# Three expert groups ranked by load and packed into 32-row lanes: sixteen expert blocks become thirteen in a decoder trunk on one Trainium2 core

## The chip, the core and the metric

The kernel runs on one core of one Trainium2 chip. The metric is device time in microseconds (us), the median of the runs shown. The engines are named as in the profile: PE is TensorE's matmul side, PEld its weight load, DVE is VectorE, ACT is ScalarE, POOL is GpSimd, SP is SyncE, whose queue issues most of the DMAs.

## What is computed

One decoder layer for 512 prompt tokens and 64 sample tokens, 576 in all, with D = 1024: a combined projection, windowed attention beside RWKV-7 time mixing, an output projection with LayerNorm, and a routed mixture of 16 experts. The change touches only the last part:

```
probs = softmax(x @ w_router);  sel = probs + router_bias        # 16 experts, 4 groups of 4
best  = the group whose two best sel have the greatest sum
idx   = the two best experts inside that group                    # 2 rows of work per token
h     = silu(x @ w_gate[e]) * (x @ w_up[e])                       # 1024 -> 512, f32
out   = sum over the two experts of weight * (h @ w_down[e])      # 512 -> 1024, f32
x     = LayerNorm(ALPHA * x + out)
```

Worked out with the reference on its own inputs, the rows that the router gives to each expert are, by group and from the most to the least loaded: 105, 91, 71, 61; then 92, 80, 73, 39; then 86, 71, 58, 53; then 91, 75, 56, 50.

## The kernel before

Up to about 530 us the projection, attention, RWKV and output projection run; then the router picks experts, and 16 expert blocks follow, one for each expert, each with room for CAP = 128 rows. Every engine runs a program of its own, ordered by semaphores.

The routing. DVE makes one-hot masks M1 and M2 of the first and second choice and hands their sum to PE ("chosen" 1). PE counts by matmul how many earlier tokens chose the same expert (L1086 and L1088). DVE turns each count into a row number (L1931 to L1935: for each choice a multiply, a reduce and a comparison with 128 row numbers, which gives a one-hot OH). PE multiplies OH by the token numbers TI (L1096, 20 matmuls), so that each slot of each expert's block learns its token, and DVE casts that to integers (L1939, "slots" 1). POOL then gathers the rows of one block at a time from HBM (L520, 0.5 MB each).

The expert blocks on PE. `gate_up(e)` (L1120) runs 8 matmuls with the gate weights and 8 with the up weights, each of 128 rows by 512 columns in f32, for which the trace shows two instructions each. `turn_xg(e+1)` (L1108) transposes the next block's rows, `down(e-1)` (L1139) multiplies the block before by its down weights, and `turn_h(e)` (L1128) transposes the hidden rows. The order in the loop is gate_up(e), turn_xg(e+1), down(e-1), turn_h(e). ACT and DVE copy and multiply what lies between, and ACT stores a block's 128 result rows to HBM (L1472).

The weights. Each expert has three matrices of 2 MB. WG, WU and WD have two buffers each, expert e uses buffer e % 2. SP issues the loads in one order written in the program (`load_expert`, L439): gate(e), up(e), down(e), gate(e+1) and so on. The loads of experts 0 and 1 are issued before the routing. Each later one first waits until the buffer's last reader is done:

```
            def load_expert(e, s, ahead=True):
...
                for nm, W, src in (("gate", WG, i_["w_gate"]), ("up", WU, i_["w_up"]), ("down", WD, i_["w_down"])):
                    if ahead:
                        sp.wait_ge(sem(nm + "_ps"), e - 1)
                    w = src[0, bass.ds(e, 1)] if ahead else src[0, e:e + 1]
```

The wait for e - 1 is over once blocks 0 to e - 2 have used that matrix. Since down(e-2) runs after gate_up(e-1), down(e), gate(e+1) and up(e+1) go out together. They have most of a block of PE's time before they are read.

After the last block POOL gathers each token's two result rows (L560), DVE combines and normalises, and SP stores the output. If an expert has more rows than its place, all engines run a loop of OVER further blocks behind a flag; with the loads above no expert has.

Of the kernel before, what the change touches and what calls it, by code (L numbers as in the profile page):

```python
# [15 lines left out]
P = 128  # L16
D = 1024
# [14 lines left out]
OVER = 2 * NT // (CAP + 1)  # L32
BLOCKS = E + OVER
# [15 lines left out]
def constant_table():  # L49
# [35 lines left out]
    t_["rank"] = np.tile(np.arange(float(P)), (P, 1))  # L85

    tok = np.arange(5)[None, :] * P + i[:, None]
    t_["tok_high"] = (tok // 32 * 32).astype(float)
    t_["tok_low"] = (tok % 32).astype(float)
    t_["iota4"] = np.tile(np.arange(4.0), (P, 1))  # L90
    t_["slot0"] = np.tile(np.arange(E) * float(CAP), (P, 1))
# [24 lines left out]
def hymba_step(nc, i_, o_):  # L116

    with ExitStack() as ctx:
# [114 lines left out]
        PR, SEL, CN, O1, O2, EQ, M1, M2, PO = (small(5, E) for _ in range(9))  # L233
# [7 lines left out]
        OH = [small(5 * P // 2).bitcast(BF16).rearrange("p (i c) -> p i c", i=5) for _ in range(2)]  # L241
        TI = [small(5 * E).bitcast(BF16).rearrange("p (i h e) -> p i h e", i=5, h=2) for _ in range(2)]
        CH = small(3 * E).bitcast(BF16).rearrange("p (i e) -> p i e", e=E)
        BEF, ONE = (small(P // 2).bitcast(BF16) for _ in range(2))
        smalli = ctx.enter_context(nc.sbuf_tensor("smalli", [P, 10 + BLOCKS + 1 + OVER], I32))
# [3 lines left out]
        eid_i = smalli[:, 11 + BLOCKS:11 + BLOCKS + OVER]  # L249
        x1d = nc.dram_tensor("x1_rows", [NT, D], F32).ap()  # L250
# [114 lines left out]
        def _(sp):  # L365
# [67 lines left out]
            def load_expert(e, s, ahead=True):  # L433

                for nm, W, src in (("gate", WG, i_["w_gate"]), ("up", WU, i_["w_up"]), ("down", WD, i_["w_down"])):
                    if ahead:
                        sp.wait_ge(sem(nm + "_ps"), e - 1)
                    w = src[0, bass.ds(e, 1)] if ahead else src[0, e:e + 1]
                    sp.dma_start(W[s], w.rearrange("a (k p) n -> p (a k) n", p=P)).then_inc(sem(f"w{nm}{s}"), 16)  # L439

            load_expert(0, 0, False)
            for i in range(5):
                if i == 1:
                    load_expert(1, 1, False)
# [11 lines left out]
            with sp.Fori(1, E // 2) as it:  # L456
                for s in range(2):
                    load_expert(2 * it + s, s)


            sp.wait_ge(sem("slots"), 2)
            more = sp.value_load(flag_i[0:1, :], min_val=0, max_val=OVER)
            with sp.If(more > 0):
                sp.wait_ge(sem("down_ps"), E)
                sp.wait_ge(sem("up_ps"), E)
# [23 lines left out]
        def _(pool):  # L489
# [5 lines left out]
            for n in range(OVER * CAP // P):  # L495
                pool.dma_start(ysd[E * CAP + n * P:E * CAP + (n + 1) * P, :], zrow).then_inc(sem("rows_zero"), 16)
# [27 lines left out]
            for e in range(E):  # L524
                gather(e)
            pool.wait_ge(sem("slots"), 2)
            more = pool.value_load(flag_i[0:1, :], min_val=0, max_val=OVER)
            with pool.If(more > 0):
# [14 lines left out]
                pool.dma_start(idx_i[0:CAP, E:BLOCKS], idxd[E * CAP:SLOTS, :].rearrange("(e p) o -> p (e o)", p=CAP),  # L543
                               allow_slow_non_contiguous=True).then_inc(sem("o_idx"), 16)
                pool.wait_ge(sem("o_idx"), 208)
                pool.wait_ge(sem("xg_turn"), E)
                for o in range(OVER):
                    if o:
                        pool.wait_ge(sem("over_pe"), 4 * o - 3)
                    pool.indirect_dma_start(out=xg[0:CAP, 0, :], out_offset=None, in_=x1d[:, :],  # L550
                                            in_offset=bass.IndirectOffsetOnAxis(ap=idx_i[0:CAP, E + o:E + o + 1], axis=0)) \
                        .then_inc(sem("o_xg"), 16)
                pool.wait_ge(sem("o_yst"), 16 * OVER)
            pool.wait_ge(sem("y_st0"), 16 * E // 2)
            pool.wait_ge(sem("y_st1"), 16 * E // 2)
            pool.wait_ge(sem("down_ps"), E)
# [15 lines left out]
        def _(pe):  # L572
# [520 lines left out]
            pe.wait_ge(sem("chosen"), 3)  # L1093
            for n in range(20):
                k, i, h = n // 10, n // 2 % 5, n % 2
                ins = mm(ps[0:CAP, 2, 0:E], OH[k][:, i, 0:CAP], TI[k][:, i, h, :], start=n == 0, stop=n == 19)  # L1096
# [5 lines left out]
            def turn_xg(e, s, first=False):  # L1102
                pe.wait_ge(sem(f"xg{s}"), e * 8 + (16 - 8 * s))
                if not first:
                    pe.wait_ge(sem("xgT_act"), e)
                    pe.wait_ge(sem("xgT_dve"), e)
                for k in range(KT):
                    ins = pe.transpose(ps[:, k // 4, (k % 4) * P:(k % 4) * P + R_], xg[0:R_, s, k * P:(k + 1) * P],  # L1108
                                       ident[0:R_, 0:R_])
                ins.then_inc(sem("xg_turn"), 1)  # L1110

            def gate_up(e, s, first=False):
                pe.wait_ge(sem("xgT_act"), e + 1)
                pe.wait_ge(sem("xgT_dve"), e + 1)
                for W, nm, b in ((WG, "gate", 2), (WU, "up", 3)):
                    pe.wait_ge(sem(f"w{nm}{s}"), e * 8 + (16 - 8 * s))
                    if not first:
                        pe.wait_ge(sem("h_ready"), e)
                    for k in range(KT):
                        ins = mm(ps[0:R_, b, :], xgT[s][:, k, 0:R_], W[s][:, k, :], start=k == 0, stop=k == KT - 1)  # L1120
                    ins.then_inc(sem(nm + "_ps"), 1)

            def turn_h(e, s, first=False):
                pe.wait_ge(sem("h_ready"), e + 1)
                if not first:
                    pe.wait_ge(sem("ht_ready"), e)
                for k in range(FT):
                    ins = pe.transpose(ps[:, 4, k * P:k * P + R_], hh[0:R_, s, k * P:(k + 1) * P], ident[0:R_, 0:R_])  # L1128
                ins.then_inc(sem("ht_ps"), 1)

            def down(e, s, first=False):
                pe.wait_ge(sem("ht_ready"), e + 1)
                pe.wait_ge(sem(f"wdown{s}"), e * 8 + (16 - 8 * s))
                if not first:
                    pe.wait_ge(sem("y_act"), e)
                    pe.wait_ge(sem("y_dve"), e)
                for h in range(2):
                    for k in range(FT):
                        ins = mm(ps[0:R_, 5 + h, :], hT[s][:, k, 0:R_], WD[s][:, k, h * 512:(h + 1) * 512],  # L1139
                                 start=k == 0, stop=k == FT - 1)  # L1140
                ins.then_inc(sem("down_ps"), 1)

            turn_xg(0, 0, True)
            gate_up(0, 0, True)
            turn_xg(1, 1)
            turn_h(0, 0, True)
            gate_up(1, 1)
            turn_xg(2, 0)
            down(0, 0, True)
            turn_h(1, 1)  # L1150
            with pe.Fori(1, E // 2 - 1) as it:
                for s in range(2):
                    e = 2 * it + s
                    gate_up(e, s)
                    turn_xg(e + 1, 1 - s)
                    down(e - 1, 1 - s)
                    turn_h(e, s)
            gate_up(E - 2, 0)
            turn_xg(E - 1, 1)
            down(E - 3, 1)  # L1160
            turn_h(E - 2, 0)
            gate_up(E - 1, 1)
            down(E - 2, 0)
            turn_h(E - 1, 1)
            down(E - 1, 1)
# [3 lines left out]
            with pe.If(more > 0):  # L1169
                pe.wait_ge(sem("y_act"), E)  # L1170
                pe.wait_ge(sem("y_dve"), E)
# [27 lines left out]
        def _(act):  # L1199
# [244 lines left out]
            def xg_copy(e, s, first=False):  # L1444
                act.wait_ge(sem("xg_turn"), e + 1)
                if not first:
                    act.wait_ge(sem("up_ps"), e - 1)
                T.up(A(xgT[s][:, 0:4, 0:R_], ps[:, 0, :].rearrange("p (k c) -> p k c", c=P)[:, :, 0:R_], ACT.Copy),  # L1448
                     "xgT_act")

            def silu(e, s, first=False):
# [639 lines left out]
```

## Time and profile before

| | us |
|---|---|
| median of 3 runs | 962.65 |
| lowest, highest | 958.43, 963.31 |
| profiled execution, its own time | 963.73 |
| its span in the trace | 961.9 |
| PE busy | 846.6 (88%) |
| first expert matmul starts | 554.87 |
| last expert matmul ends | 910.45 |

The span is what the trace covers; the profiled execution's own time is 1.8 us longer. A row of the chain of waits gives a start, a duration and the work that everything behind it waited for. A row of the timeline gives for merged instructions the start, the time up to the last end, the tile of the array (rows*columns), the shape and the count. Ends of matmuls are modelled and overlap the next start, so distances are taken from start to start. In a row of the stretches the last three numbers are the granted TensorE clock as a share of 2.4 GHz, the busy share of the DMA engines, and GB/s.

### The profile page before, as it was taken

What the parts mean: (1) busy time and instruction counts of PE and PEld (TensorE: products, weight loads), DVE (VectorE), ACT (ScalarE), POOL (GpSimd) and SP (SyncE); (2) the same over time, 40 slices, a digit from 0 to 9 for tenths busy, and PEclk for the clock granted to TensorE, in tenths of its full rate; (3) what the DMA queues carried; (4) which work ended last, traced back from release to release, by engine and by line L of the source; (5) the groups of instructions that cost most, each with busy time, mean ns of one, the idle gap of its engine ahead of it and who ended that gap; (6) DMA issues with size and microseconds to landing.
All of it is one profiled execution on the core that took longest, in us unless ns stands there. A gap on an engine that the chain in (4) does not pass through costs nothing.

```text
span 961.9 us, 14926 instructions
## 1 busy us (share of the span) xinstructions
PE 846.6 (88%) x6437; PEld 526.5 (55%) x6437; DVE 354.8 (37%) x643; ACT 191.1 (20%) x409; POOL 72.4 (8%) x69
## 2 busy tenths in 40 slices
PE   5999999999997999889998399999999999999700
PEld 4776776766886898654453244444444444444300
DVE  1000477687456554478345630000010010000057
ACT  1221244433322223313000010100010011001102
POOL 0010000000000000133100000000000000000065
PEclk7999999999798999999999589999999999999955
DMA  9361211000700000005890254999999989988152
GB/s 323 91 237 48 71 44 39 6 1 1 210 3 2 15 4 3 2 1 115 307 359 30 88 171 133 339 342 341 341 339 337 340 310 326 337 310 314 45 196 98
DMA packets 68351, 159.22 MB, mean 166 GB/s; under 512 B 12596, under 2 KB 15156, under 8 KB 68036
## 3 DMA queue, kind: packets, MB, share of 16 engines
q1 hardware_dynamic: 60560, 130.27, 39.1%
q0 software_dynamic: 4768, 17.30, 5.0%
q10 hardware_dynamic: 2964, 10.78, 2.8%
q8 instruction: 47, 0.77, 0.3%
q14 instruction: 12, 0.10, 0.0%
HBM read 139.67 MB, written 18.71 MB: 165 GB/s over the span
## 4 chain that ended last, share of the span: by engine, by line
PE 80%; DVE 10%; ACT 3%; DMA 3%; issue 2%; POOL 1%; ACTq 0%; DVEq 0%; POOLq 0%
PE ps L1120 23%; PE ps L598 14%; PE ps L1139 11%; PE ps L1009 7%; PE ps L807 2%; PE ps L791 2%; PE ps L1108 2%; PE ps L825 2%; PE ps L779 1%; PE ps L645 1%; DVE arena L1644 1%; PE ps L754 1%; PE ps L617 1%; PE ps L1065 1%; POOL arena L560 1%
## 5 line engine op out<-in xcount | busy, mean ns | idle before, releaser
L1120 PE MATMUL ps<-arena 128*128 128x512 f32 x512 | 225.7, 598 | 1.1 <-ACT arena L1448 1.1
L598 PE MATMUL ps<-arena 128*128 128x256 f32 (+1 forms) x640 | 164.7, 416 | 0.6 <-ACT arena L1212 0.6
L1120 PEld LDWEIGHTS ps<-arena 128*128 128x128 f32 x512 | 96.7, 191 | 119.0 <-issue 117.3
L598 PEld LDWEIGHTS ps<-arena 128*128 128x128 f32 x640 | 121.5, 192 | 35.8 <-ACT arena L1212 0.8
L1139 PE MATMUL ps<-arena 128*128 128x512 f32 x256 | 112.6, 592 | 1.5 <-ACT arena L1461 1.5
L1980 DVE TENSOR_TENSOR arena<-arena,ps 128x512 f32<-128x512 f32 x16 | 11.0, 689 | 213.6 <-PE ps L1120 213.6
L1139 PEld LDWEIGHTS ps<-arena 128*128 128x128 f32 x256 | 47.2, 189 | 56.1 <-issue 54.3
L1009 PE MATMUL ps<-arena 128*128 128x512 f32 (+1 forms) x160 | 69.8, 593 | 0.0
L1009 PEld LDWEIGHTS ps<-arena 128*128 128x128 f32 (+1 forms) x160 | 28.0, 178 | 37.8 <-issue 37.2
L1986 DVE COPY arena<-ps 128x512 f32<-128x512 f32 x16 | 11.1, 692 | 101.9 <-PE ps L1139 101.9
L520 POOL DMA_INDIRECT arena<-x_rows,smalli x16 | 15.1, 942 | 355.4 <-PE ps L1108 267.6
L1448 ACT ACTIVATE arena<-ps 128x512 f32<-128x512 f32 x16 | 9.6, 599 | 124.9 <-PE ps L1108 124.9
L807 PE MATMUL ps<-arena 64*64 64x64 f32 x672 | 29.1, 221 | 4.0 <-DVE arena L1734 3.8
L503 POOL TENSOR_TENSOR arena<-arena 128x512 f32<-128x512 f32 x4 | 4.7, 1165 | 359.6 <-ACT arena L1387 359.6
L1455 ACT ACTIVATE arena<-ps 128x512 f32<-128x512 f32 x16 | 9.6, 598 | 97.2 <-PE ps L1120 97.2
L791 PE MATMUL ps<-arena 64*64 64x64 f32 x672 | 28.6, 221 | 0.0
L1461 ACT ACTIVATE arena<-ps 128x512 f32<-128x512 f32 x16 | 9.6, 599 | 94.6 <-PE ps L1128 93.9
L1357 ACT ACTIVATE arena<-ps 128x256 f32<-128x256 f32 (+1 forms) x44 | 16.5, 375 | 58.8 <-PE ps L791 58.8
L807 PEld LDWEIGHTS ps<-arena 64*64 64x64 f32 x672 | 25.0, 136 | 5.0 <-DVE arena L1734 4.8
L791 PEld LDWEIGHTS ps<-arena 64*64 64x64 f32 x672 | 24.9, 137 | 0.2
L1260 ACT ACTIVATE arena<-arena,att_st 128x256 f32<-128x256 f32 (+1 forms) x36 | 17.6, 491 | 35.4 <-DVE att_st L1601 35.4
L1108 PEld LDWEIGHTS ps<-arena 128*128 128x128 f32 x128 | 15.6, 146 | 12.9 <-issue 7.9
(298 smaller groups left out, 1016.8 us busy)
## 6 DMA issues: line engine op xcount, KB each, us to landing
arena<-in_w_gate SPq DMA_DIRECT2D x16, 2048.0 KB, 14.4
arena<-in_w_up SPq DMA_DIRECT2D x16, 2048.0 KB, 20.5
arena<-in_w_down SPq DMA_DIRECT2D x16, 2048.0 KB, 9.9
arena<-in_win SPq DMA_DIRECT2D x20, 512.0 KB, 3.5
expert_rows<-arena ACTq DMA_DIRECT2D x16, 512.0 KB, 8.4
expert_rows<-arena POOLq DMA_DIRECT2D x8, 512.0 KB, 6.7
arena<-in_wo SPq DMA_DIRECT2D x1, 4096.0 KB, 12.3
arena<-in_x_prompt ACTq DMA_DIRECT2D x4, 512.0 KB, 8.1
```

The source lines that it names most:

```text
L520: pool.indirect_dma_start(out=xg[0:CAP, e % 2, :], out_offset=None, in_=x1d[:, :], in_offset=bass.IndirectOffsetOnAxis(ap=idx_i[0:CAP, e:e ...
L598: ins = mm(ps[:, bank_of[part, ct], 0:n], ring[:, ct % RING, k, :], xT[:, k, lo:lo + n], start=k == 0, stop=k == KT - 1)
L791: ins = mm(ps[r, bank, c], X[g][r, c], ident[r, r], start=True, stop=True)
L807: ins = mm(ps[r, 4 + g, c], BG[g][r, s * P + 64:(s + 1) * P], X[g][r, c], start=True, stop=True)
L825: ins = mm(ps[r, 6 + g, c], XT[g][r, c], W1[g][r, c], start=True, stop=True)
L1009: ins = mm(ps[0:r, 4 + 2 * (i % 2) + h, :], m, wo[:, k, h * 512:(h + 1) * 512], start=k == 0, stop=k == KT - 1)
L1108: ins = pe.transpose(ps[:, k // 4, (k % 4) * P:(k % 4) * P + R_], xg[0:R_, s, k * P:(k + 1) * P], ident[0:R_, 0:R_])
L1120: ins = mm(ps[0:R_, b, :], xgT[s][:, k, 0:R_], W[s][:, k, :], start=k == 0, stop=k == KT - 1)
L1139: ins = mm(ps[0:R_, 5 + h, :], hT[s][:, k, 0:R_], WD[s][:, k, h * 512:(h + 1) * 512], start=k == 0, stop=k == FT - 1)
L1260: A(Sn[:, g, :], Sn[:, g, :], ACT.Exp, bias=st[:, 1, g:g + 1], accum_out=st[:, 3, g:g + 1])
L1357: T.up(A(XT[g][:, 0:W], ps[:, bank, 0:W], ACT.Copy), "xt2_ev")
L1986: T.up(dve.tensor_copy(yst[0:R_, s, 512:D], ps[0:R_, 6, :]), "y_dve")
```

## The change

The 16 blocks become NBLK = 13. Experts 0 to 3 keep a block of 128 rows each, in their order. In each of the other three groups DVE ranks the four experts by their number of rows, and three blocks of four 32-row lanes take them: block 1 the most loaded (4 lanes, 128 rows), block 2 the second in 3 lanes and one lane of the third, block 3 two more lanes of the third and two lanes of the fourth. The places are thus 128, 96, 96 and 64 rows. Below, x stands for a turn (x = 4g + rank), b for a block; turn x uses buffer x % 2.

A shared block needs the weights of two experts. A matmul then covers only the columns of the array that belong to an expert's lanes and reads that expert's weights: `tiles(b)` cuts lanes into pieces of 64 and 32 columns (3 lanes make 64 + 32). So blocks 5, 8 and 11 run for each of the 24 steps (8 gate, 8 up, 8 down) a piece of 64 and two of 32 columns, and blocks 6, 9 and 12 two of 64.

SP reads the expert of a turn from a table that DVE now writes (`turn_i`), waits for "slots" 2 ahead of turn 4, and loads turn x into the buffer of turn x - 2 once the last block that uses that turn, LAST[x - 2], is done. LAST is 0 to 4 for turns 0 to 4, then 5, 6, 6 for turns 5 to 7, 7, 8, 9, 9 for 8 to 11 and 10, 11, 12, 12 for 12 to 15. Turns 8 and 9, and 12 and 13, are loaded as pairs: both gates, both ups, both downs. OVER rises from 8 to 12, and with it the zero rows that POOL writes early on.

```diff
-OVER = 2 * NT // (CAP + 1)
-BLOCKS = E + OVER
+LANE = 32
+OVER = 12
+def block_lanes():
+    blocks = [[(x, 0, 4)] for x in range(4)]
+    for g in range(1, 4):
+        a = 4 * g
+        blocks += [[(a, 0, 4)], [(a + 1, 0, 3), (a + 2, 3, 4)], [(a + 2, 0, 2), (a + 3, 2, 4)]]
+    return blocks
+LANES = block_lanes()
+NBLK = len(LANES)
+LAST = {x: b for b, lanes in enumerate(LANES) for x, _, _ in lanes}
...
-            with sp.Fori(1, E // 2) as it:
-                for s in range(2):
-                    load_expert(2 * it + s, s)
+            def load_turn(x, nm, e):
+                W, src = {"gate": (WG, i_["w_gate"]), "up": (WU, i_["w_up"]), "down": (WD, i_["w_down"])}[nm]
+                sp.wait_ge(sem(nm + "_ps"), LAST[x - 2] + 1)
+                w = src[0, e:e + 1] if isinstance(e, int) else src[0, bass.ds(e, 1)]
+                sp.dma_start(W[x % 2], w.rearrange("a (k p) n -> p (a k) n", p=P)).then_inc(sem(f"w{nm}{x % 2}"), 16)
+            for x in (2, 3):
+                for nm in ("gate", "up", "down"):
+                    load_turn(x, nm, x)
+            sp.wait_ge(sem("slots"), 2)
+            for pair in ((4, ), (5, ), (6, ), (7, ), (8, 9), (10, ), (11, ), (12, 13), (14, ), (15, )):
+                ids = [sp.value_load(turn_i[0:1, x:x + 1], min_val=0, max_val=E - 1) for x in pair]
+                for nm in ("gate", "up", "down"):
+                    for x, e in zip(pair, ids):
+                        load_turn(x, nm, e)
...
+            def tiles(b):
+                out = []
+                for x, lo, hi in LANES[b]:
+                    cuts = [lo, hi] if hi - lo != 3 else [lo, lo + 2, hi]
+                    out += [(x, LANE * m, LANE * n) for m, n in zip(cuts, cuts[1:])]
+                return out
...
+            def gate_up(b):
...
+                for W, nm, bank in ((WG, "gate", 2), (WU, "up", 3)):
+                    for x, _, _ in LANES[b]:
+                        pe.wait_ge(sem(f"w{nm}{x % 2}"), 16 * (x // 2 + 1))
...
+                    for k in range(KT):
+                        for x, lo, hi in tiles(b):
+                            ins = mm(ps[lo:hi, bank, :], xgT[b % 2][:, k, lo:hi], W[x % 2][:, k, :],
+                                     start=k == 0, stop=k == KT - 1)
...
+            L(TT(KEY, KEY, C("load_tie"), ALU.add))
+            L(TT(T64, by_group(KEY).unsqueeze(2).to_broadcast([P, 4, 4, 4]),
+                 by_group(KEY).unsqueeze(3).to_broadcast([P, 4, 4, 4]), ALU.is_gt))
+            L(dve.tensor_reduce(RNK, T64.rearrange("p g e f -> p (g e) f"), AX, ALU.add))
...
+            T.up(TT(OH, C("rank").unsqueeze(1).to_broadcast([P, 10, P]), ROW.unsqueeze(2).to_broadcast([P, 10, P]),
+                    ALU.is_equal), "chosen")
...
+            dve.tensor_copy(turn_i, KEY)
             dve.wait_ge(sem("route_ps"), 2)
-            T.up(dve.tensor_copy(idx_i[0:CAP, 0:E], ps[0:CAP, 2, 0:E]), "slots")
+            T.up(dve.tensor_copy(idx_i[0:CAP, 0:NBLK], ps[0:CAP, 2, 0:NBLK]), "slots")
```

SP's order in the changed program, from the loads of turn 5 to the first of turn 7 (the TENSOR_LOAD reads the expert's number, and the ISA row in front of a gate load waits for its buffer):

```order
L491 DMA arena<-in_w_gate 128x8x512
L491 DMA arena<-in_w_up 128x8x512 [waits up_ps]
L491 DMA arena<-in_w_down 128x4x1024 [waits down_ps]
L498 TENSOR_LOAD smalli
L498 ISA x2
L491 ISA [waits gate_ps]
L491 DMA arena<-in_w_gate 128x8x512
L491 DMA arena<-in_w_up 128x8x512 [waits up_ps]
L491 DMA arena<-in_w_down 128x4x1024 [waits down_ps]
```

The order of gate, up, down is the one of before. What moved is the reader: turn 6's gate load now feeds block 5, where expert 6's fed block 6.

PE's order in the changed program from the end of block 4's iteration into block 5 (L1195 is down, L1181 turn_h, L1172 gate_up; wgate0 and wgate1 are the landings in the two gate buffers):

```order
L1195 MATMUL ps<-arena 128x512 [waits y_act,y_dve,wdown1,ht_ready]
L1195 MATMUL ps<-arena 128x512 x7
L1181 MATMUL ps<-arena 128x128 [waits ht_ready,h_ready]
L1181 MATMUL ps<-arena 128x128 x3
L1172 MATMUL ps<-arena 64x512 [waits wgate0,wgate1,h_ready,xgT_dve,xgT_act]
L1172 MATMUL ps<-arena 32x512 x2
L1172 MATMUL ps<-arena 64x512
L1172 MATMUL ps<-arena 32x512 x2
```

Block 5 begins right behind down(3), waits for both gate buffers, and alternates between pieces of 64 and 32 columns, where before 16 matmuls of 128 columns stood.

## Rows read from the trace of the kernel before

**Rows 1.** The page: span, PE's share, the chain's shares by engine.

```profile
span 961.9 us, 14926 instructions
PE 846.6 (88%) x6437; PEld 526.5 (55%) x6437; DVE 354.8 (37%) x643; ACT 191.1 (20%) x409; POOL 72.4 (8%) x69
PE 80%; DVE 10%; ACT 3%; DMA 3%; issue 2%; POOL 1%; ACTq 0%; DVEq 0%; POOLq 0%
```

**Rows 2.** The chain of waits from 554 us: start, duration, work.

```profile
554.87 16.73 PE ps L1120 x32
...
588.18 6.87 PE ps L1139 x16
595.05 0.44 PE ps L1128 x4
595.48 13.77 PE ps L1120 x32
609.25 0.87 PE ps L1108 x8
...
894.51 6.88 PE ps L1139 x16
...
903.30 7.15 PE ps L1139 x16
```

**Rows 3.** The stretches 600 to 640 us and 680 to 720 us.

```profile
600.00:640.00 40.00, 40.00 (x112) 18.88 (x111) 4.14 (x6) 4.07 (x8) 1.87 (x2) 1.00 0.92 340
...
680.00:720.00 40.00, 40.00 (x112) 18.88 (x111) 3.58 (x6) 4.09 (x8) 0.94 (x1) 1.00 0.91 330
```

**Rows 4.** SP's timeline, 594 to 618 us: its issues.

```profile
595.08 0.37 SPq L439 DMA_DIRECT2D arena<-in_w_down  x1
595.66 0.38 SPq L439 DMA_DIRECT2D arena<-in_w_gate  x1
596.13 5.73 SPq L439 DMA_DIRECT2D arena<-in_w_up  x1
617.02 0.37 SPq L439 DMA_DIRECT2D arena<-in_w_down  x1
```

**Rows 5.** The page's DMA issues: KB each, median us from issue to landing.

```profile
arena<-in_w_gate SPq DMA_DIRECT2D x16, 2048.0 KB, 14.4
arena<-in_w_up SPq DMA_DIRECT2D x16, 2048.0 KB, 20.5
arena<-in_w_down SPq DMA_DIRECT2D x16, 2048.0 KB, 9.9
```

**Rows 6.** Groups by line and form: small tiles of the array, busy us, mean ns.

```profile
L656 PE MATMUL ps<-arena 64*32 64x128 f32 x32 | 1.3, 276 | 0.0
...
L657 PE MATMUL ps<-arena 64*32 64x64 f32 x32 | 1.2, 214 | 0.0
```

**Rows 7.** PE's timeline at 399 us (64*64 tiles, 512 columns streamed).

```profile
398.99 1.93 PE L897 MATMUL ps<-arena 64*64 64x512 f32 x8 [0.79 <-ACT arena L1384]
```

**Rows 8.** PE's timeline at 136 and 208 us, where the tile form changes.

```profile
136.50 0.64 PE L680 MATMUL ps<-arena 128*64 128x512 f32 x1
...
136.98 0.59 PE L680 MATMUL ps<-arena 128*64 128x512 f32 x1
137.41 0.59 PE L681 MATMUL ps<-arena 128*64 128x512 f32 x1
...
208.65 0.59 PE L681 MATMUL ps<-arena 128*64 128x512 f32 x1
209.17 0.44 PE L656 MATMUL ps<-arena 64*32 64x128 f32 x8
```

**Rows 9.** PE's timeline at 248 us: L687 and L688 alternate.

```profile
248.23 0.30 PE L688 MATMUL ps<-arena 64*64 64x32 f32 x2
248.46 0.30 PE L687 MATMUL ps<-arena 128*64 128x32 f32 x2
248.69 0.30 PE L688 MATMUL ps<-arena 64*64 64x32 f32 x2
```

**Rows 10.** The stretches around the first expert block.

```profile
540.00:554.90 14.90, 3.16 (x35) 2.61 (x35) 10.47 (x43) 0.88 (x2) 2.63 (x3) 0.50 0.23 70
554.90:560.40 5.50, 5.50 (x7) 2.40 (x8) 4.97 (x18) 1.00 (x1) 0.28 (x1) 0.50 0.32 95
560.40:575.00 14.60, 14.40 (x42) 6.81 (x42) 2.77 (x5) 1.80 (x3) 0.94 (x1) 1.00 0.59 183
```

**Rows 11.** DVE's timeline in the routing.

```profile
543.50 0.24 DVE L1931 COPY arena<-ps 128x80 f32<-128x80 f32 x1
543.77 0.24 DVE L1933 TENSOR_TENSOR arena<-arena 128x80 f32<-128x80 f32 x1
...
545.60 0.82 DVE L1935 TENSOR_TENSOR arena<-arena 128x640 bf16<-128x640 f32 x1
```

**Rows 12.** SP's read of a value (the group of line L462).

```profile
L462 SPq TENSOR_LOAD <-smalli x1: 488/488/488, 880.9 to 880.9; - x1
```

More of the change, by code:

```diff
@@ L232, in hymba_step @@
         zidx = ctx.enter_context(nc.sbuf_tensor("zidx", [P, BLOCKS], I32))
-        PR, SEL, CN, O1, O2, EQ, M1, M2, PO = (small(5, E) for _ in range(9))
+        PR, SEL, CN, O1, O2, EQ, W5, OV, PO = (small(5, E) for _ in range(9))
+        M12, EQ2 = small(10, E), small(10, E)
+        M1, M2 = M12[:, 0:5, :], M12[:, 5:10, :]
+        GEB = small(10, NBLK + 1)
+        POS, NBK, ROW = small(10), small(10), small(10)
+        KEY, RNK, GA, GC, SL = (small(E) for _ in range(5))
+        T64 = small(4, 4, 4)
+        BLK = small(10, NBLK)
         G1, G2, C1, SC, BGR, CNB = (small(5, 4) for _ in range(6))
@@ L522, in gather @@
                     .then_inc(sem(f"xg{e % 2}"), 16)
-            for e in range(E):
+            for e in range(NBLK):
                 gather(e)
@@ L1112, in gate_up @@
[L1112 to L1128, printed above, removed]
-                ins.then_inc(sem("ht_ps"), 1)
[L1131 to L1136, printed above, removed]
+            def tiles(b):
[4 more added lines that the diff above has]
+                return out
@@ new lines, in turn_h, with down @@
+            def turn_h(b):
+                pe.wait_ge(sem("h_ready"), b + 1)
+                if b:
+                    pe.wait_ge(sem("ht_ready"), b)
+                for k in range(FT):
+                    ins = pe.transpose(ps[:, 4, k * P:k * P + R_], hh[0:R_, b % 2, k * P:(k + 1) * P],
+                                       ident[0:R_, 0:R_])
+                ins.then_inc(sem("ht_ps"), 1)
+            def down(b):
+                pe.wait_ge(sem("ht_ready"), b + 1)
+                for x, _, _ in LANES[b]:
+                    pe.wait_ge(sem(f"wdown{x % 2}"), 16 * (x // 2 + 1))
+                if b:
+                    pe.wait_ge(sem("y_act"), b)
+                    pe.wait_ge(sem("y_dve"), b)
@@ L1137, in down @@
                 for h in range(2):
                     for k in range(FT):
-                        ins = mm(ps[0:R_, 5 + h, :], hT[s][:, k, 0:R_], WD[s][:, k, h * 512:(h + 1) * 512],
-                                 start=k == 0, stop=k == FT - 1)
+                        for x, lo, hi in tiles(b):
+                            ins = mm(ps[lo:hi, 5 + h, :], hT[b % 2][:, k, lo:hi], WD[x % 2][:, k, h * 512:(h + 1) * 512],
+                                     start=k == 0, stop=k == FT - 1)
                 ins.then_inc(sem("down_ps"), 1)
-            turn_xg(0, 0, True)
@@ L1144, in _ @@
[L1144 to L1165, printed above, removed]
+            turn_xg(0)
+            for b in range(NBLK):
+                gate_up(b)
+                if b + 1 < NBLK:
+                    turn_xg(b + 1)
+                if b:
+                    down(b - 1)
+                turn_h(b)
+            down(NBLK - 1)
             pe.wait_ge(sem("slots"), 2)
@@ L1505, in _ @@
+            for b in range(NBLK):
+                silu(b)
+                if b + 1 < NBLK:
+                    xg_copy(b + 1)
+                if b and b + 1 == NBLK:
+                    y_copy(b - 1)
+                h_copy(b)
+                if b and b + 1 < NBLK:
+                    y_copy(b - 1)
+            y_copy(NBLK - 1)
             act.wait_ge(sem("slots"), 2)
@@ new lines, in _ @@
+            L(dve.tensor_reduce(POS, EQ2, AX, ALU.add))
+            L(TT(GEB, POS.unsqueeze(2).to_broadcast([P, 10, NBLK + 1]),
+                 C("block0").unsqueeze(1).to_broadcast([P, 10, NBLK + 1]), ALU.is_ge))
+            TT(BLK, GEB[:, :, 0:NBLK], GEB[:, :, 1:NBLK + 1], ALU.subtract)
+            L(dve.tensor_reduce(NBK, GEB, AX, ALU.add))
+            for h, part in enumerate(("tok_high", "tok_low")):
+                TT(TI[:, :, h, :], BLK, C(part).unsqueeze(2).to_broadcast([P, 10, NBLK]), ALU.mult)
```

274 lines of the change are left out of this document (125 added, 149 removed).

## The prediction

> **What bounds the kernel now.** I read the page first, then the chain of waits, the stretches, SP's timeline, and last PE's timeline where small tiles of the array run. The page shows PE busy for 88% of the span, and the chain that ended last is PE's for 80% [rows 1]. In the expert part the chain is PE alone: a block is 13.77 (gate and up) + 0.87 + 6.87 (down) + 0.44 = 21.95 us [rows 2], sixteen times, from 554.87 to 910.45. PE is never idle there and has its full clock [rows 3]. DMA stands close behind: engines 0.91 to 0.92 busy at 330 to 340 GB/s [rows 3]. So fewer blocks save PE's time only as far as the same 16 sets of weights still arrive in time, and the question is what each load waits for.
>
> **Blocks removed.** 16 - 13 = 3 blocks of 21.95 us: **-65.8 us**, if a shared block costs PE what a full one does. Two things speak on that.
>
> **Do pieces of the array run side by side?** Eight instructions on two 64*64 tiles take 1.93 us [rows 7]. One instruction of 512 columns takes 13.77 / 32 = 0.43 us [rows 2]; in a row eight would take 3.44, two at a time 1.72 and a pipeline end. They ran two at a time, although both instructions of one matmul were issued ahead of the next tile's. L656 and L657, on four column tiles, stay busy 1.3 us for 32 + 32 instructions of 128 and 64 columns [rows 6]; by 0.87 / 8 = 0.11 us for 128 columns [rows 2] they would need 5.2 us in turn. So pieces of equal size overlap, also where each streams its own data, and blocks 6, 9 and 12 (64 + 64) cost about a full block. No row shows this with 128 rows. Bounds: nothing, or the second piece in turn, 24 x 0.86 = 20.6 us a block. I take nothing; the rows of small tiles are the nearest.
>
> **Pieces of unequal size.** Where the form of the tile changes, the trace shows a gap: between L681 (128*64) and L656 (64*32) 208.65 to 209.17 = 0.52 us instead of 0.43, and the first instruction of a new form holds 136.50 to 136.98 = 0.48 us, its weight load uncovered [rows 8]. L687 and L688 alternate between two forms every two instructions, and a turn takes 0.23 us for 32 columns [rows 9]. At 248.46 the new tile has columns 64 to 127 while the old one had 0 to 63: nothing in common, and the same 0.23 as at 248.69. So the change of form itself is waited for, not a conflict. In blocks 5, 8 and 11 each step is a 64 piece, then two 32 pieces: 0.48 + 0.52 = 1.00 us for the first, and 1.00 for the two together. 2.00 - 0.86 = 1.14 us more a step, 3 x 24 = 72 steps: **+82 us**. No row shows 64 beside 32 columns with equal rows; the bounds are nothing (1073 in all, a rival below) and three pieces in turn, 2 x 72 x 0.86 plus the gaps, about +144. I take +82. "Changing tiling mode (not just tile) drains the TensorE", says the Trainium skill (TensorEngine Tiling (Array Packing), section Tiling Modes, Key Properties), and it lists 128×64 and 128×32 as two modes; by it the sum is 1155, and by the same page's statement that tiles operate independently alone it would be 1073. Entering and leaving column tiles in the 64 + 64 blocks: some six changes of 0.1 us a block, **+2 us**.
>
> **The loads, the largest term.** SP is one queue and takes its waits in order. Before, down(e) waits for down(e-2), which PE runs behind gate_up(e-1); at that moment down, gate and up go out at 595.08, 595.66 and 596.13 [rows 4] and land 9.9, 14.4 and 20.5 us later [rows 5]. The gate lands at 610.1 and is read a block later, at 617.4. In the changed kernel the readers come a block sooner. Turn 6 feeds block 5, but its gate load stands behind turn 5's down load, which waits for down(3), the second last thing ahead of block 5. So PE reaches gate_up(5) at the point that corresponds to 595.48 [rows 2] and stands until 595.66 + 14.4 = 610.06: **14.6 us**. The same holds for block 6 (turn 7 behind down 6), 9 (11 behind down 10) and 12 (15 behind down 14): 4 x 14.6 = 58.4. Blocks 8 and 11 need the third transfer behind the wait (down 8, down 9, gate 10): 596.13 + 20.5 - 595.48 = 21.15, twice: 42.3. Blocks 7 and 10 need the second transfer for gate, but their up is the fourth (down, gate, gate, up): third minus second is 6.6 us and second minus first 5.1, so it lands about 27 us after the start, where PE asks at 14.6 + 6.9 + 3 (its clock, below) = 24.5: 14.6 + 2.5, twice: 34.2. The last block's down (turn 15) waits for down(11) and lands 9.9 us later, where before down(15) started 903.30 - 901.39 = 1.9 us behind the down ahead of it [rows 2]: 8.0. Together **+142.9 us**. The stalls don't shrink in longer blocks, since each starts at the end of a down. Bounds for one gate stall: a gate alone in the queue can't beat the 9.9 us of a load that goes first, so 9 us, and 15 with the value read (0.49 us [rows 12]) uncovered; over nine places 90 to 160. The value reads stand behind a down load that is still moving 2 MB, so I cost them at nothing; uncovered, ten times 0.7 us.
>
> **PE's clock.** During 546 to 554 PE was nearly idle, and the granted clock was 0.50 (1.2 GHz) until 560.4 [rows 10]. The first block's gate and up took 16.73 instead of 13.77 us [rows 2]: 2.96 us for one start from the low level. Each of nine stalls has at least 8 us without a matmul: **+26.7 us**; 0 to 4 us each as bounds.
>
> **Routing.** DVE now runs 24 instructions between the counts and OH, where seven stood. Small ones step by 0.27 us (543.50 to 543.77), 640 elements take 0.82 [rows 11]. Some 23 at 0.2 to 0.35 come to 5.5, OH with 1280 elements to 1.45, so 6.95 against 2.9; four TI products leave the front, of which 0.5 us was exposed: **+3.6 us** on the path to the first gather. Turn_i's four instructions hide under PE's 20 matmuls; without that cover, 0.9. The longer tail to "slots" 2 ends near 560, and turn 4 is loaded near 600. POOL's four more zero writes (2 MB) fall in the projection, which PE bounds; uncovered they'd cost about 6 us.
>
> **The sum.** 961.9 - 65.8 + 82.1 + 2 + 142.9 + 26.7 + 3.6 = 1153.4 as a span; the profiled execution's own time is 1.8 above its span, so **1155 us**. It stands 1.1 us above the median of the runs shown, which I leave out.
>
> **Rivals.**
> Unequal pieces side by side (0.20). The form counts by rows only and 64 + 32 + 32 columns overlap as in [rows 6]. For it: the gaps seen include a change of rows or overlapping columns. 1155 - 82 = 1073 us; stalls as forecast.
> No overlap with 128 rows (0.06). Streams of 128 rows for two pieces compete: 20.6 us more in three blocks of 64 + 64 and in three of 64 + 32 + 32: 1155 + 124 = 1279 us. Against it: [rows 7].
> Loads hidden, forms dear (0.04): 1155 - 143 - 27 = 985 us.
> The other side (0.03): faster. Its place is the gate load of a shared block. If it lands before gate_up asks, the stalls and the clock's share go, and with pieces side by side 1155 - 170 - 82 = 903 us remain. For it: DMA would move its bytes in time, 296 us for 16 sets (100.7 MB) at the rate of [rows 3], against 285 of PE. It decides where SP issues the gate load at least 14.6 us ahead of the end of down(b-1). Against it: the order shows the down wait in front of it, and [rows 4] SP standing from 596 to 617 behind such a wait.
> More rows than room (0.03): the change doesn't do what it says. If an expert exceeds 128, 96, 96 or 64 rows, twelve further blocks of at least 22 us run: over 1400 us. The loads worked out from the reference (92, 80, 73, 39 at most by rank) fit.
> The forecast itself has 0.64.
>
> **How the numbers follow.** The range holds the forecast with its bounds and the first rival: 1062 to 1185. Left out are the others, and tails. About 0.5% is what a measurement of this kernel can tell from no change. Only the other side is faster, 0.03; a mixture could end at no change, 0.01; the rest, 0.96, is slower.
>
> **What would show it.** In the profile after: eight idle stretches on PE ahead of gate_up in blocks 5 to 12, of about 15 or 21 us, ended by in_w_gate landings, with SP's down and gate issues 0.6 us apart at their start; one of 8 ahead of the last down; granted clock 0.50 for some 5 us behind each. DMA's mean share falls well under 0.9. L1172 with 64 and 32 columns: 16 us for gate alone against 7. Blocks 6, 9 and 12 at 6.9. If L1172's 32-column instructions overlap those of 64, the form term is wrong; if PE never waits for in_w_gate, the load term is, and with it most of the forecast.

## The result

| | changed kernel, us | kernel before, us |
|---|---|---|
| median | 1147.45 (4 runs) | 960.74 (4 runs) |
| lowest to highest | 1145.03 to 1150.99 | 958.43 to 963.31 |
| span of the profiled execution | 1143.2 | 961.9 |

The ratio is 1.1932, 95% interval 1.1901 to 1.1963. The changed kernel is slower by 186.7 us. The forecast was 1155, and as a span 1153.4. The profiled execution was the fastest of the four, 2.4 us below their median.

The page of the changed kernel: span, PE's share, the granted clock over 40 slices, the chain's shares, and DMA's issues.

```profile
span 1143.2 us, 15263 instructions
PE 880.6 (77%) x6689; PEld 489.3 (43%) x6689; DVE 352.0 (31%) x651; ACT 184.2 (16%) x397; POOL 71.4 (6%) x70
...
PEclk8999999989999999996699979797788879797865
...
PE 69%; DMA 15%; DVE 8%; ACT 3%; issue 2%; SPq 1%; POOL 1%; ACTq 0%; DVEq 0%
...
arena<-in_w_gate SPq DMA_DIRECT2D x16, 2048.0 KB, 14.2
arena<-in_w_up SPq DMA_DIRECT2D x16, 2048.0 KB, 20.2
arena<-in_w_down SPq DMA_DIRECT2D x16, 2048.0 KB, 9.9
```

Before, the chain had 3% of DMA and 80% of PE [rows 1]; now DMA has 15%. The loads themselves take what they took [rows 5]. In the expert part PE had no wait for weights before. Here are its waits between 540 and 1100 us in the changed kernel: who waited for whom, us in total, how often, the longest.

```profile
PE ps L1172 <- DMA arena<-in_w_gate: 131.1, 8, 20.2
PE ps L1195 <- DMA arena<-in_w_down: 9.7, 1, 9.7
...
PE ps L1172 <- DMA arena<-in_w_up: 4.4, 2, 2.7
```

145.2 us in all: eight gate waits, two for up, one for the last down, as many as the prediction has and in the same places. The chain of waits shows the first two, at blocks 5 and 6.

```profile
640.67 13.76 PE ps L1172 x32
654.44 0.87 PE ps L1158 x8
655.31 6.88 PE ps L1195 x16
662.21 0.37 SPq L491
662.62 0.27 SPq L498
662.92 0.15 SPq L498
...
663.34 14.22 DMA arena<-in_w_gate
677.56 0.25 issue
677.81 33.46 PE ps L1172 x96
711.26 1.02 PE ps L1158 x8
712.29 6.88 PE ps L1195 x16
719.19 0.37 SPq L491
...
720.31 14.12 DMA arena<-in_w_gate
734.43 0.25 issue
734.67 16.25 PE ps L1172 x64
750.92 1.02 PE ps L1158 x8
751.95 15.90 PE ps L1195 x48
```

Block 4 is a full block, as in [rows 2]. Then down(3) ends at 662.2, and only there does SP go on: it issues a down load, reads the expert's number (L498) and issues the gate load, which takes 14.2 us to its landing, while PE stands. Block 5's gate and up (64 + 32 + 32 columns) take 33.46 us where block 4's took 13.76, its down (751.95) 15.90 in place of 6.88. Block 6's gate and up, 64 + 64 columns, take 16.25.

A step of block 5 in PE's timeline. Each row is a short window of its own: its count takes in all instructions that run in the window, also the next ones that have begun, and its tile is that of the first:

```profile
697.30 1.07 PE L1172 MATMUL ps<-arena 128*64 128x512 f32 x2
697.78 1.15 PE L1172 MATMUL ps<-arena 128*64 128x512 f32 x3
698.30 1.05 PE L1172 MATMUL ps<-arena 128*32 128x512 f32 x4
698.75 1.17 PE L1172 MATMUL ps<-arena 128*32 128x512 f32 x3
```

The starts are what counts. 697.30 and 697.78 are the two instructions of the 64 piece, 0.48 us apart. The 32 pieces follow after 0.52 us, four instructions in two pairs, 0.45 apart, so that both 32 pieces run together. 0.48 and 0.52 are the intervals of [rows 8].

And the stretches from the wait ahead of block 6 to its matmuls (columns as in [rows 3]):

```profile
720.00:735.00 15.00, 0.33 (x2) 0.32 (x4) 0.00 (x0) 0.71 (x2) 0.00 (x0) 0.57 0.98 356
735.00:751.00 16.00, 16.00 (x65) 5.32 (x62) 0.00 (x0) 0.60 (x1) 0.00 (x0) 0.87 0.26 94
```

During the wait PE is idle and DMA full; behind it DMA is nearly idle (0.26) and PE still has only 0.87 of its clock.

### The profile page after: what moved, and what is told of

It is laid out like the page before. It is cut to its first block, busy times and chain, and to the rows that moved or that the text cites. A ratio compares the mean times of both kernels' runs of the same rounds, so it can differ in the third digit from the quotient of the medians.

```text
span 1143.2 us, 15263 instructions
## 1 busy us (share of the span) xinstructions
PE 880.6 (77%) x6689; PEld 489.3 (43%) x6689; DVE 352.0 (31%) x651; ACT 184.2 (16%) x397; POOL 71.4 (6%) x70
## 4 chain that ended last, share of the span: by engine, by line
PE 69%; DMA 15%; DVE 8%; ACT 3%; issue 2%; SPq 1%; POOL 1%; ACTq 0%; DVEq 0%
PE ps L1172 21%; PE ps L640 12%; PE ps L1195 10%; DMA arena<-in_w_gate 8%; PE ps L1051 6%; DMA arena<-in_w_up 4%; PE ps L849 2%; PE ps L833 2%; PE ps L867 1%; PE ps L1158 1%; PE ps L821 1%; SPq L491 1%; PE ps L687 1%; DVE arena L1665 1%; DMA arena<-in_w_down 1%
## 5 line engine op out<-in xcount | busy, mean ns | idle before, releaser
L1172 PE MATMUL ps<-arena 128*32 128x512 f32 (+2 forms) x704 | 255.3, 645 | 136.6 <-DMA arena<-in_w_gate 131.1
L1172 PEld LDWEIGHTS ps<-arena 128*32 128x32 f32 (+2 forms) x704 | 77.5, 156 | 306.1 <-issue 298.3
L640 PEld LDWEIGHTS ps<-arena 128*128 128x128 f32 x640 | 120.8, 191 | 35.5 <-ACT arena L1254 0.8
L1195 PE MATMUL ps<-arena 128*32 128x512 f32 (+2 forms) x352 | 120.1, 611 | 9.7 <-DMA arena<-in_w_down 9.7
L1195 PEld LDWEIGHTS ps<-arena 128*32 128x32 f32 (+2 forms) x352 | 36.0, 148 | 84.9 <-issue 84.9
L1497 ACT ACTIVATE arena<-ps 128x512 f32<-128x512 f32 x13 | 7.8, 598 | 255.6 <-PE ps L1172 255.6
L562 POOL DMA_INDIRECT arena<-x_rows,smalli x13 | 12.3, 944 | 436.2 <-PE ps L1158 345.4
L849 PE MATMUL ps<-arena 64*64 64x64 f32 x672 | 29.1, 222 | 4.0 <-DVE arena L1755 3.8
L1490 ACT ACTIVATE arena<-ps 128x512 f32<-128x512 f32 x13 | 7.8, 598 | 139.9 <-PE ps L1158 139.9
L833 PE MATMUL ps<-arena 64*64 64x64 f32 x672 | 28.6, 221 | 0.0
L1503 ACT ACTIVATE arena<-ps 128x512 f32<-128x512 f32 x13 | 7.8, 598 | 93.4 <-PE ps L1181 92.7
L867 PE MATMUL ps<-arena 64*64 64x64 f32 x528 | 21.6, 225 | 1.1
## 6 DMA issues: line engine op xcount, KB each, us to landing
arena<-in_w_gate SPq DMA_DIRECT2D x16, 2048.0 KB, 14.2
arena<-in_w_up SPq DMA_DIRECT2D x16, 2048.0 KB, 20.2
```

The costliest lines, as they stand in the source:

```text
L562: pool.indirect_dma_start(out=xg[0:CAP, e % 2, :], out_offset=None, in_=x1d[:, :], in_offset=bass.IndirectOffsetOnAxis(ap=idx_i[0:CAP, e:e ...
L640: ins = mm(ps[:, bank_of[part, ct], 0:n], ring[:, ct % RING, k, :], xT[:, k, lo:lo + n], start=k == 0, stop=k == KT - 1)
L833: ins = mm(ps[r, bank, c], X[g][r, c], ident[r, r], start=True, stop=True)
L849: ins = mm(ps[r, 4 + g, c], BG[g][r, s * P + 64:(s + 1) * P], X[g][r, c], start=True, stop=True)
L867: ins = mm(ps[r, 6 + g, c], XT[g][r, c], W1[g][r, c], start=True, stop=True)
L1172: ins = mm(ps[lo:hi, bank, :], xgT[b % 2][:, k, lo:hi], W[x % 2][:, k, :], start=k == 0, stop=k == KT - 1)
```

## The experiments

Each experiment stands beside runs of the kernel before on its own chip. These had a median of 963.69 us beside e1, e2, e3 and e6, 963.43 beside e5, e7 and e8, and 961.53 beside e9. The changed kernel's own were at 960.74, so a difference from its median can be off by some 3 us. The traces give a second measure, the expert part alone. It is 79.2 us shorter than in the changed kernel in e1, 14.5 in e5 and 154.1 in e2, where the medians say 81.4, 17.7 and 155.4.

The theory is three costs, each by itself: pieces of unequal form (82 us), SP's order (some 145 us), and the clock behind each wait.

**e1: one form in the blocks of 3 + 1 lanes.**

```diff
-                for x, lo, hi in LANES[b]:
-                    cuts = [lo, hi] if hi - lo != 3 else [lo, lo + 2, hi]
+                even = all(hi - lo != 3 for _, lo, hi in LANES[b])
+                for x, lo, hi in LANES[b]:
+                    cuts = [lo, hi] if even else list(range(lo, hi + 1))
```

> The changed kernel with the pieces of blocks 5, 8 and 11 cut into four of 32 columns, one form, instead of 64 + 32 + 32. My theory (a change of the tile's form makes PE drain, pieces of one form overlap): a step falls from 1.99 to about 0.86 us, 72 steps, so 81 us less: 1066 us, with the waits for weights unchanged near 145 us. Rival A (the cost is in running several streams of 128 rows at once, not in the change of form): four pieces cost as much as three or more, 1147 us or above. Rival B (pieces of 32 columns overlap only two at a time): 72 x 1.72, about 1128 us.

Measured: 1066.09 us (1.1057 of the kernel before, 1.0997 to 1.1117), 81.4 below the changed kernel's median. PE's timeline at block 5, gate and up:

```profile
677.57 15.84 PE L1173 MATMUL ps<-arena 128*32 128x512 f32 x128 [15.05 <-DMA arena<-in_w_gate]
```

128 instructions of 512 columns in 15.84 us: four at a time (in turn they would need 55). PE now issues more instructions, 128 in place of 96, and takes half as long. So it was neither the number of pieces nor the streams of 128 rows that cost the time, but the unequal forms. The wait ahead of it, 15.05 us, stays, and with it a low clock: without a wait the same 128 instructions take 13.90 us (e3).

**e5: the same unequal pieces, but the form changes once in a matrix.**

```diff
-                    for k in range(KT):
-                        for x, lo, hi in tiles(b):
+                    for form in forms(b):
+                        for k in range(KT):
+                            for x, lo, hi in form:
```

Here `forms(b)` is the pieces of 64 columns, then those of 32; down is reordered alike.

> The changed kernel with the same 64 + 32 + 32 pieces in blocks 5, 8 and 11, but all steps of the 64 piece first and then all steps of the 32 pieces, so that the form changes once in a matrix (gate, up or down) and not twice in each step. My theory (each change of form costs a drain of 0.09 us and an uncovered weight load, and unequal forms never overlap): a matrix of such a block falls from 15.9 to 2 x 6.88 and a little, 13.95 us, nine of them, 17 us less: 1130 us. Rival (it is the drains alone; pieces of unequal form overlap once they stand apart): down to about 7 us a matrix, 1067 us. Rival (the order in a step costs nothing, the two forms simply compute in turn): no change, 1147 us.

Measured: 1129.77 us (1.1736, 1.1697 to 1.1775), 17.7 less than the changed kernel. Block 5:

```profile
678.89 29.82 PE L1177 MATMUL ps<-arena 128*64 128x512 f32 x96 [15.26 <-DMA arena<-in_w_gate]
```

29.82 for gate and up against 33.46. Both have a low clock at their start. The block's down has none:

```profile
749.59 14.03 PE ps L1201 x48
```

It took 15.90 us in the changed kernel: 1.87 us less for each of nine matrices, 17 in all. So the 82 us split: some 17 lie in the gaps at each change of form, and some 64 are left, since unequal forms compute in turn. Sparing the changes is thus not enough. e5 offers the unequal pieces to PE one after the other and can't tell by itself whether they could overlap. That they don't is read from the step above, where 64 and 32 columns with nothing in common alternate and still follow each other by 0.52 us, and e1 shows that equal pieces remove the cost.

**e2: only SP's order.**

```diff
-            for pair in ((4, ), (5, ), (6, ), (7, ), (8, 9), (10, ), (11, ), (12, 13), (14, ), (15, )):
...
+            def free_at(x, nm):
+                b = LAST[x - 2]
+                return {"gate": (b, 0), "up": (b, 1), "down": (b + 1, 2)}[nm]
+            for x, nm in sorted(((x, nm) for x in range(2, E) for nm in ("gate", "up", "down")),
+                                key=lambda a: free_at(*a)):
```

Loads go out in the order in which PE frees their buffers: the gate of turn 6 ahead of the down load of turn 5. The number of an expert is read just ahead of its first load.

> The changed kernel with only SP's order of the loads changed: each load is issued in the order in which its buffer comes free on PE (gate and up of a turn ahead of the down load before it). Pieces stay 64 + 32 + 32. My theory (SP stands in front of a down load's wait while gate buffers are free): of 145 us of waits for weights some 6 stay, and the clock's share goes with them: about 985 us. Rival (DMA has not the bandwidth for the shared blocks): the waits move and at least half of them stay, 1060 us or more.

Measured: 992.04 us (1.0299, 1.0263 to 1.0334), 155.4 less. Of PE's waits for weights in the expert part one is left (first fence). SP's timeline shows three of its issues (second fence):

```profile
PE ps L1198 <- DMA arena<-in_w_down: 9.6, 1, 9.6
```

```profile
646.76 0.38 SPq L491 DMA_DIRECT2D arena<-in_w_gate  x1
653.50 0.37 SPq L491 DMA_DIRECT2D arena<-in_w_up  x1
661.24 0.37 SPq L491 DMA_DIRECT2D arena<-in_w_down  x1
```

Here 646.76 is turn 6's gate, 653.50 its up, 661.24 the down of turn 5: the gate goes out 14.5 us ahead of the down it stood behind. DMA had the bandwidth; the bytes are the same. With blocks this long the loads are hidden again, apart from the last. The low clock goes with the waits, so that e2 also shows what blocks 5 and 6 cost without it: gate and up take 31.76 and 13.92 us.

```profile
661.65 31.76 PE ps L1175 x96
...
701.74 13.92 PE ps L1175 x64
```

**e6: matmuls in place of the idle time.**

```diff
+                if b >= 5:
+                    for _ in range(FILL[b]):
+                        mm(ps[:, 7, 0:P], ident, ident, start=True, stop=True)
                 gate_up(b)
```

FILL is 88 for blocks 8 and 11 and 60 for the other six.

> The changed kernel with matmuls of the identity into an unused PSUM bank just ahead of gate_up in blocks 5 to 12 (60 of them, 88 ahead of blocks 8 and 11): they fill most of each wait and change nothing else. My theory (each wait also drops PE's granted clock to half, which then costs about 2 us of the next matmuls): the eight waits end when they did, the blocks behind them run at full clock, some 16 us less: 1131 us. Rival (the waits cost their own length alone): 1147 us; it comes out higher if the filler lasts longer than a wait.

Measured: 1144.50 us (1.1881, 1.1840 to 1.1921), less than I expected: the interval overlaps that of the changed kernel. PE's timeline, block 5 and block 7:

```profile
661.78 13.56 PE L1204 MATMUL ps<-arena 128*128 128x128 f32 x120
677.02 31.80 PE L1172 MATMUL ps<-arena 128*64 128x512 f32 x96 [1.68 <-DMA arena<-in_w_gate]
...
779.06 7.12 PE L1172 MATMUL ps<-arena 128*128 128x512 f32 x16 [1.94 <-DMA arena<-in_w_gate]
790.51 9.65 PE L1172 MATMUL ps<-arena 128*128 128x512 f32 x16 [4.33 <-DMA arena<-in_w_up]
```

In blocks 5, 6, 8, 9 and 11 the theory holds: with the filler, gate and up take 31.80 us in place of 33.46 in block 5, 13.98 for 16.25 in block 6, 31.80 for 33.66 in block 8, 13.99 for 16.36 in block 9 and 31.80 for 34.18 in block 11. That is 1.7 to 2.4 us of clock behind a wait. Block 12 gains only 0.9 us. In blocks 7 and 10 the filler gives time back: gate starts at full clock and ends sooner, so PE waits 4.33 us for up instead of 2.72, and the up matrix then takes 9.65 us where the changed kernel took 7.15. The stretch 787 to 797 us has a granted clock of 0.66:

```profile
787.00:797.00 10.00, 6.49 (x10) 2.77 (x11) 0.00 (x0) 0.00 (x0) 0.00 (x0) 0.66 0.71 265
```

Blocks 7 and 10 thus end 2.7 and 3.2 us later after the down ahead of them than in the changed kernel. And the gate loads did not land when they had: ahead of blocks 8, 9, 11 and 12 PE's gate matmuls began 0.8 to 1.4 us later after the end of the down before, some 4 us together (8: 21.74 against 20.79; 12: 16.98 against 15.57). Why those loads took longer was not tried. The clock term is real in the blocks, but the run's total doesn't show it, and "16 us less" was wrong.

**e8: SP's order alone, in the kernel before.**

```diff
-            with sp.Fori(1, E // 2) as it:
-                for s in range(2):
-                    load_expert(2 * it + s, s)
+            free_at = {"gate": 0, "up": 1, "down": 5}
+            for e, nm in sorted(((e, nm) for e in range(2, E) for nm in ("gate", "up", "down")),
+                                key=lambda a: 3 * (a[0] - 2) + free_at[a[1]]):
```

> The kernel before with its loads in the order in which buffers come free, written out instead of the loop, blocks unchanged. My theory (in the kernel before no block waits for weights, since each load has a block of PE's time): no change, within 0.5%, 961 us, so that what the reordered version gains over the kernel before comes from its three fewer blocks. Rival (the order is worth something by itself, because DMA works more evenly): 950 us or less.

Measured: 963.11 us, ratio 1.0005 (0.9971 to 1.0040): nothing. The order is worth something in the changed kernel, where a reader comes a block sooner, and nothing in this one.

**e3: e1 and e2 together.**

> Both edits together: one form in the shared blocks and the loads in the order in which buffers come free. My theory: 13 blocks of 21.95 us, with 11 to 25 us of waits because DMA must bring 4 sets in each 66 us of three blocks: 911 to 925 us, below the kernel before. Rival (with PE this fast DMA is the bound, at 340 GB/s as in the kernel before): the 16 sets, gathers and stores take about 330 us in place of 286, 945 us or more, little under the kernel before.

Measured: 925.23 us, 0.9594 of the kernel before (0.9557 to 0.9630), at the upper end of what was expected. Both costs gone, the three blocks saved show: 38 us less. Block 5's gate and up now take what a full block's do, within 0.14 us:

```profile
666.10 13.90 PE ps L1176 x124
```

Waits in the expert part: 9.7 us for the last down, 2.8 for up, 0.7 for gate, and 5.4 in blocks 7 and 10 that the trace gives to "issue" ahead of down. These too are waits for weights: in e7, which has the same one of 2.70 us in block 7, the down load is issued at 706.11 and lands 20.3 us later, at 726.4, and PE goes on at 726.58.

**e7: e3, and the last down load into a free gate buffer.**

```diff
+                if (x, nm) == (E - 1, "down"):
+                    sp.wait_ge(sem("gate_ps"), NBLK)
+                    sp.dma_start(LAST_DOWN, src[0, bass.ds(e, 1)].rearrange("a (k p) n -> p (a k) n", p=P)) \
+                      .then_inc(sem("wdown1"), 16)
```

> The version with one form and the reordered loads, and in addition the last turn's down weights go into the first gate buffer, which is free once the last block's gate matmuls are done, and not into the down buffer of turn 13. My theory: the 9.7 us wait ahead of the last down goes, and with it some 1.5 us of half clock behind it: 11 us less than that version, 914 us. Rival (the load then collides with the last up and down loads, and only moves the wait): 920 us or more.

Measured: 911.89 us, 0.9482 of the kernel before (0.9445 to 0.9520), 13.3 less than e3. The last wait for weights is gone. Not all of the 13.3 us is shown to be the edit's. In the two profiled executions the expert part is 8.4 us shorter (304.1 against 312.5), where 11 were expected, and the rest is that it begins at 555.1 instead of 560.9. In the eight traces with the new routing that start lies anywhere between these two. What remains, and the stretch around blocks 7 and 8:

```profile
PE ps L1184 <- DMA arena<-in_w_up: 4.5, 2, 2.3
PE ps L1208 <- issue: 3.7, 2, 2.7
...
PE ps L1184 <- DMA arena<-in_w_gate: 0.5, 1, 0.5
```

```profile
740.00:780.00 40.00, 39.51 (x246) 15.48 (x239) 4.05 (x6) 3.86 (x7) 1.88 (x2) 1.00 1.03 393
```

**e9: e7, with turns 9 and 13 behind the down load that is read first.**

```diff
-                return {"gate": (b, 0), "up": (b, 1), "down": (b + 1, 2)}[nm]
+                late = 3 if x in (9, 13) else 0
+                return {"gate": (b, late), "up": (b, late + (not late)), "down": (b + 1, 2)}[nm]
```

> The version with one form, the reordered loads and the moved last load, and in addition the gate and up loads of turns 9 and 13 are issued behind the down load of turns 7 and 11: both are free at the same time, but the down load is read first. In the version without this edit PE still waits 8.7 us for weights around blocks 7 and 10 (4.5 for up, 3.7 for down, 0.5 for gate). My theory (those waits come from the order in the queue, not from DMA's bandwidth): most of them go, 904 to 907 us against 911.9. Rival (DMA is the bound in this stretch, at over 380 GB/s): the waits move to blocks 8 and 11 and the time stays at 910 us or more.

Measured: 918.15 us (0.9531, 0.9496 to 0.9565): the theory fell, its rival held. PE's waits:

```profile
PE ps L1185 <- DMA arena<-in_w_gate: 12.6, 2, 8.1
```

```profile
700.00:740.00 40.00, 32.12 (x158) 12.88 (x154) 4.14 (x6) 3.96 (x7) 1.87 (x2) 0.94 1.00 364
```

The two gate waits, ahead of blocks 8 and 11, took the place of 8.7 us around blocks 7 and 10, and the blocks behind them have a low clock (16.42 and 15.26 us for 13.90). The expert part is 309.2 us against 304.1 in e7. The same stretch, 700 to 740 us, of e7:

```profile
700.00:740.00 40.00, 34.96 (x196) 13.65 (x188) 2.76 (x4) 3.37 (x6) 1.20 (x2) 1.00 1.04 389
```

In this stretch the DMA engines are busy throughout in both orders, but with the loads held back they moved 364 GB/s instead of 389. What was held back was paid ahead of blocks 8 and 11. That DMA binds the shared blocks as much as PE does, once the forms are equal and the loads hidden, fits these rows but is not shown by them alone: no run had more bandwidth, or fewer bytes.

## Why the prediction was right

The expert part ran from 554.87 to 910.45 before and from 556.08 to 1092.65 in the changed kernel: 355.6 and 536.6 us, 181.0 more. The measured terms without routing, which lies ahead of that part, come to 180.5. The terms, as forecast and as measured:

| term | forecast | measured | from |
|---|---|---|---|
| three blocks fewer | -65.8 | -65.8 | blocks 0 to 4 keep 21.95 us |
| unequal pieces | +82.1 | +81 | 15.90 / 8 - 0.86 = 1.13 us a step, 72 steps; e1: 81.4 less |
| entering and leaving column tiles | +2 | about +2.5 | in 64 + 64 blocks down 7.04 against 6.88, gate and up 13.98 (e6) against 13.77; next to any column pieces turn_xg 1.02 against 0.87, turn_h 0.59 against 0.44 (e2) |
| waits for weights | +142.9 | +143.8 | PE's waits, 145.2, less what stood at the last down before; e2: 155.4 less, clock included |
| clock behind the waits | +26.7 | about +19 | below |
| routing | +3.6 | +3.0 | below |

**The loads.** The forecast worked each wait out from three landings of one moment [rows 4, 5], and it held place by place. Six gate waits were 15.0 to 15.2 us against 14.6, two were 20.1 and 20.2 against 21.15: together 131.1 against 129.9, with errors of opposite sign. Two waits for up came to 4.4 against 5. The last down waited 9.7 us, but 1.9 us lay between the last two downs before as well; down to down it is 10.2 - 1.9 = 8.3 more, against 8.0. The value reads, which the forecast put at nothing, cost at most 0.4 us each: from the down load's issue to the gate's landing it is 663.34 + 14.22 - 662.21 = 15.35 us, and 595.66 + 14.4 - 595.08 = 14.98 before. e2 shows the cause: the same loads in another order leave only the last wait.

**The pieces.** The choice between two rows was right. [Rows 9] had shown that a change of form is waited for even where the tiles have nothing in common, but there the number of rows changed; in the changed kernel it is the columns alone, and the intervals are the same 0.48 and 0.52 us. The Trainium skill (TensorEngine Tiling (Array Packing), section Tiling Modes, Key Properties) says that changing the tiling mode, and not just the tile, drains the TensorE. By it the sum was 1155, and the trace agrees: 0.52 us to the first instruction of the other form, where equal ones follow after 0.43. The rivals are out: unequal pieces side by side (1073) by the step of 1.99 us, and no overlap with 128 rows (1279) by e1 and by blocks 6 and 9. Equal pieces overlap two and four at a time with 128 rows too, which no row of before had shown.

**The clock** is the term that was mis-sized: 2.96 us for each of nine places came from the start of the first block [rows 10]. Measured against e6, which has no low clock there, blocks 5, 6, 8 and 9 lost 1.66, 2.27, 1.86 and 2.37 us; e2, with a granted clock of 1.00 from 620 to 920 us, has the same 31.8 and 13.9. Against the same 31.80 and 13.98, blocks 11 and 12 lost 2.4 and 2.6 (34.18 and 16.61). Gate in blocks 7 and 10 took 8.9 where e6 took 7.1, and the last down 8.94 us against 7.04: 1.8 to 1.9 each. Together 18.7. Most waits thus cost about two thirds of the forecast. The cost is no constant: behind the last wait, which is 9.6 to 9.7 us in each, down took 8.94 us here, 8.45 in e3 and 10.02 in e1, which is 1.4 to 3.0 above 7.04. The forecast had one row for it, and that row lies at the upper end. What sets the size within this range was not tried.

```profile
1003.15 10.02 PE ps L1196 x32
```

The missing 8 us are most of the 10.2 us by which the span stayed below the forecast (1143.2 against 1153.4). Another 2 us come from the parts ahead of the routing (below). The median stands 7.5 us below 1155 and not 10 because the profiled execution was the fastest of the four.

**The routing.** From the last mask of the choice (L1924 before, L1945 after, the same instruction) to the first gather it is 541.97 to 547.75, 5.8 us, and 539.87 to 548.67, 8.8: 3.0 more against 3.6. The chain shows DVE's OH with 1280 elements at 1.50 us, where 1.45 was forecast. The parts ahead of it happened to be 2 us faster in this execution, so the first expert matmul is only 1.2 us later; in the eight traces with the new routing it starts anywhere from 555.1 to 560.9.

**The other side** (903 us, chance 0.03) did not come about, but its mechanism was sound: with the gate load issued 14.5 us ahead (e2) the waits go, and with both costs removed e3 gives 925 us; e7, which also moves the last load, gives 912. What e7 misses to 903 is in the main its 8.7 us of waits. The rival's own numbers had room for them: it held that DMA would move its bytes in time, with 296 us for 16 sets against 285 of PE, though 296 is the larger. And it compared only over the whole part: in a group of three blocks DMA must bring four sets, 25.2 MB, in 66 us, which is some 380 GB/s.

## What to carry to other kernels

When two sets of weights share one block, ask of each load not only how much bandwidth there is but which wait stands ahead of it in its queue: the queue here held gate loads back behind a down load's wait once their reader came a block sooner, and sorting by the moment at which each buffer comes free gave 155 us without a byte less. Pieces of 64 and of 32 columns did not share a step of the matmul array, while pieces of one shape did. So cut the wide ones down to the narrowest: four pieces of 32 took 13.90 us where one of 128 takes 13.76. A saving of three blocks in sixteen was buried under both, so look in the trace at what the removed work had hidden before counting it.

## What was not expected

The length of a short wait did not decide whether PE's clock fell. In the changed kernel a wait of 2.72 us between gate and up of block 7 left the following 16 instructions at 7.15 us; in e6 a wait of 4.33 us at the same place, 7 us of matmuls after the one of 1.94 us, brought the granted clock to 0.66 over ten us, and they took 9.65. A filler that kept the clock up through a long wait thus lost it in a short one behind. Other traces show that a still shorter wait can do it. In e7 PE waited 2.34 us for up in block 7, and the 16 instructions behind took 7.15; in block 10 it waited 2.17 us and they took 8.84, with a granted clock of 0.60 from 791 to 794 us:

```profile
788.63 8.84 PE L1184 MATMUL ps<-arena 128*128 128x512 f32 x16 [2.17 <-DMA arena<-in_w_up]
```

Why one fell and the other didn't was not tried.

With the DMA engines' busy share at 1.03 to 1.04, the core's transfers ran at 389 to 393 GB/s (e7), against 330 to 340 in [rows 3], where PE set the pace.
